# Retention: input rows multiplied by the decayed scores before the value weights

## The reference

```python
ql, kl, vl = h_lat @ Wq, h_lat @ Wk, h_lat @ Wv      # 256, 256 and 512 columns
kc, vc     = h_ctx @ Wk, h_ctx @ Wv
# chunked scans forward and backward, which come to
S   = [ql @ kc.T , ql @ kl.T] * decay                # 256 x 512, decay from the two rates of the head
ret = S @ [vc ; vl]                                  # 256 x 512
r   = head_rms(ret) * silu(h_lat @ Wg)
```

## Time and profile before

| | us |
|---|---|
| median of 3 runs | 2317.76 |
| lowest and highest | 2315.4, 2329.35 |
| profiled execution, device time | 2323.94 |
| its span in the trace | 2322.1 |
| PE busy in the span | 2205.8 (95%) |
| DVE busy | 464.5 (20%) |
| ACT busy | 344.1 (15%) |
| granted TensorE clock, mean | 0.965 of full |

### The profile page before, as it was taken

The page is one execution under the profiler, slowest core; times in us unless marked ns, Lnnn a source line. Parts: engine busy times, 40 slices in busy tenths (PEclk is TensorE's granted clock), DMA queues, the critical chain, the costliest instruction groups (busy, mean ns, idle before and its releaser), DMA issues.

```text
span 2322.1 us, 22897 instructions
## 1 busy us (share of the span) xinstructions
PE 2205.8 (95%) x9001; PEld 925.5 (40%) x9001; DVE 464.5 (20%) x1021; ACT 344.1 (15%) x515; POOL 53.0 (2%) x64
## 2 busy tenths in 40 slices
PE   8988999999999999999999999999999999999997
PEld 6655433222225444445455533333333333333332
DVE  0124311111112301101034132222222212112113
ACT  1321111111111022210114111111111111111111
POOL 1001100000000000000000010000000000000000
PEclk9969799999999999999999989999999999999999
DMA  9484399999999322124240259999999999999994
GB/s 339 162 326 199 156 429 427 428 429 428 428 429 351 109 91 91 50 86 152 93 149 38 84 215 428 428 428 418 429 428 428 427 422 426 429 423 426 429 421 205
DMA packets 88153, 713.17 MB, mean 307 GB/s; under 512 B 6091, under 2 KB 8384, under 8 KB 50832
## 3 DMA queue, kind: packets, MB, share of 16 engines
q1 hardware_dynamic: 86112, 707.20, 73.8%
q0 software_dynamic: 2000, 5.41, 0.7%
HBM read 711.53 MB, written 1.06 MB: 307 GB/s over the span
## 4 chain that ended last, share of the span: by engine, by line
PE 81%; DMA 13%; ACT 3%; DVE 2%; issue 1%; ACTq 0%; DVEq 0%; SPq 0%; POOLq 0%; POOL 0%
PE bank L678 19%; PE bank L668 17%; PE bank L401 14%; DMA ring<-in_w_up 12%; PE bank L389 4%; PE bank L430 4%; PE bank L648 3%; PE bank L685 3%; PE bank L660 3%; PE bank L417 2%; ACT pool L1314 2%; PE bank L859 1%; PE bank L493 1%; PE bank L653 1%; PE bank L980 1%
## 5 line engine op out<-in xcount | busy, mean ns | idle before, releaser
L668 PE MATMUL bank<-ring,pool 128*64 128x512 f32 x2560 | 593.0, 616 | 26.2 <-DMA ring<-in_w_up 22.7
L678 PE MATMUL bank<-ring,pool 128*64 128x512 f32 x2048 | 448.1, 595 | 0.8 <-DVE pool L1834 0.8
L668 PEld LDWEIGHTS bank<-ring,pool 128*64 128x64 f32 x2560 | 182.0, 141 | 411.6 <-issue 365.8
L401 PE MATMUL bank<-ring,pool 128*128 128x512 f32 (+2 forms) x800 | 333.6, 578 | 5.4 <-DVE pool L1950 3.8
L678 PEld LDWEIGHTS bank<-ring,pool 128*64 128x64 f32 x2048 | 144.4, 137 | 281.5 <-issue 279.9
L401 PEld LDWEIGHTS bank<-ring,pool 128*128 128x128 f32 x800 | 152.3, 191 | 181.2 <-issue 167.5
L1208 ACT ACTIVATE pool<-bank 128x512 f32<-128x512 f32 (+1 forms) x125 | 72.9, 583 | 488.7 <-PE bank L401 174.9
L685 PE MATMUL bank<-pool,junk 64*128 64x512 f32 x400 | 99.4, 615 | 1.4 <-ACT pool L1329 1.4
L1900 DVE TENSOR_SCALAR pool<-bank 128x512 f32<-128x512 f32 x32 | 22.1, 692 | 387.5 <-PE bank L678 387.5
L648 PE MATMUL bank<-pool 128*64 128x512 f32 x384 | 96.5, 624 | 2.7 <-DVE pool L1830 2.7
L1911 DVE COPY junk<-bank 128x256 f32<-128x256 f32 x48 | 20.4, 424 | 389.2 <-PE bank L699 389.2
(11 more groups left out here) (345 smaller groups left out, 1380.2 us busy)
## 6 DMA issues: line engine op xcount, KB each, us to landing
ring<-in_exp_w_gu SPq DMA_DIRECT2D x128, 2048.0 KB, 13.7
ring<-in_exp_w_down SPq DMA_DIRECT2D x64, 2048.0 KB, 9.9
ring<-in_w_gate SPq DMA_DIRECT2D x32, 2048.0 KB, 23.6
ring<-in_w_up SPq DMA_DIRECT2D x32, 2048.0 KB, 25.6
ring<-in_w_down SPq DMA_DIRECT2D x32, 2048.0 KB, 21.4
ring<-in_w_in SPq DMA_DIRECT2D x22, 2048.0 KB, 14.4
ring<-in_ada_w SPq DMA_DIRECT2D x12, 2048.0 KB, 11.4
ring<-in_w_out SPq DMA_DIRECT2D x4, 2048.0 KB, 15.6
```

What stands on the lines that cost most here:

```text
L401: i = mm(ps[:, 0:width], src[:, k, t * P:(t + 1) * P], w[:, k, 0:width], start=(k == 0), stop=(k == w.shape[1] - 1))
L668: i = mm(dst[half[f], :], chunks[kk], weights[j][:, k, f * 512:(f + 1) * 512], start=(kk == 0), stop=(kk == KC - 1))
L678: i = mm(dst[half[f], :], chunks[2 * j + k], weights[j][:, k, at:at + 512], start=False, stop=(j == 3 and k == 1))
```

## The change

Per head, the 512 input rows are multiplied by the decayed scores first (`u`, transposed: 8 chunks of 128 columns of `D`, each over 4 blocks of 128 tokens, moving operand `dec2` of 256 columns), ACT copies `u` to `uT`, and `ro` is `uT` times the value weights (2 tiles of 8 matmuls of 512 columns). The value product `rv` of all 512 tokens is gone.

The input rows are needed with tokens on the partitions: `turn_back` transposes `ctxT` (`hc`) and `latT` (`hl`) back, 16 transposes each, and ACT copies them to `in_rows`. They lie in ring slot 5 for the time of phase `b`, which therefore streams through five slots (`PLACE`); the first expert load of `m2` into that slot waits for the last `u` (`unit_done["rows", 0]`). Gate units come before value units in the stream. The scores of head h+1 and their decays are made ahead of `ro` of head h.

```diff
-            at = (FIRST_SLOT[phase] + n) % SLOTS
+            at = PLACE[phase][n % len(PLACE[phase])]
...
-        rv = [B(7 + i).rearrange("p (j c) -> p j c", j=4) for i in range(2)]
+        uT = [B(7 + i).rearrange("p (k t) -> p k t", k=KC) for i in range(2)]
+        in_rows = ring[:, 5 * SLOT:6 * SLOT].rearrange("p (j d) -> p j d", j=4)
...
         for h in range(RH):
+            unit_b(("rg", h), cols(w2, OFF["rg"] + RV * h, RV), 8, RV)
             unit_b(("rv", h), cols(w2, OFF["rv"] + RV * h, RV), 8, RV)
-            unit_b(("rg", h), cols(w2, OFF["rg"] + RV * h, RV), 8, RV)
...
-        FIRST_SLOT = {"a": 0, "m1": len(units_a), "b": len(units_a), "m2": len(units_a) + len(units_b)}
+        PLACE = {"a": (0, 1, 2, 3, 4, 5), "m1": (2, 3, 4, 5, 0, 1), "b": (2, 3, 4, 0, 1), "m2": (5, 1, 2, 3, 4, 0)}
+        BEFORE = {"a": {}, "m1": {j: ("a", len(units_a) - 6 + j) for j in range(SLOTS)},
+                  "b": {n: ("m1", j) for n, j in enumerate((0, 1, 2, 4, 5))},
+                  "m2": {j: ("b", len(units_b) - 6 + j) for j in range(1, SLOTS)}}
...
+            def turn_back(name, srcT):
+
+                for t in range(TC):
+                    for g in range(2):
+                        ps = open_tile(pe, (name, t, g))
+                        for c in range(4):
+                            i = tp(ps[:, c * P:(c + 1) * P], srcT[:, 4 * g + c, t * P:(t + 1) * P], ident)
+                        filled(i, (name, t, g))
+
             pe.wait_ge(S("ctxT_ready"), 8)
             for u in range(2):
                 n = UB["rk", u]
                 by_columns(("kc", u), "b", n, part("b", n, KC, 512), ctxT, last=False)
+            turn_back("hc", ctxT)
             pe.wait_ge(*stage("xn_ready"))
             transposes("lT", xn_rows, 4)
...
+            turn_back("hl", latT)
             pe.wait_ge(S("rotated"), 4)
             transposes("rkT", rk_rows, 4)
...
-            for h in range(RH):
-                n = UB["rv", h]
-                by_rows([("rv", h, j) for j in range(4)], "b", n, part("b", n, KC, RV), both, RV)
+            def scores(h):
                 for jp in range(2):
                     ps = open_tile(pe, ("S", h, jp))
...
+            scores(0)
+            for h in range(RH):
                 n = UB["rg", h]
                 by_rows([("rg", h, t) for t in range(TC)], "b", n, part("b", n, KC, RV), [(latT, t) for t in range(TC)], RV)
-                pe.wait_ge(S("rv_ready"), 4 * (h + 1))
+                if h == 0:
+                    pe.wait_ge(S("in_rows_ready"), 8)
                 pe.wait_ge(S("ret_weights"), 2 * (h + 1))
+                for g in range(4):
+                    ps = open_tile(pe, ("u", h, g))
+                    for c in range(2):
+                        k = 2 * g + c
+                        for j in range(4):
+                            i = mm(ps[:, c * T:(c + 1) * T], in_rows[:, j, k * P:(k + 1) * P], dec2[:, j, :], start=(j == 0), stop=(j == 3))
+                    filled(i, ("u", h, g))
+                if h + 1 < RH:
+                    scores(h + 1)
+                n = UB["rv", h]
+                landed("b", n)
+                w = part("b", n, KC, RV)
+                pe.wait_ge(S("uT_ready"), 4 * h + 4)
                 for t in range(TC):
                     ps = open_tile(pe, ("ro", h, t))
-                    for j in range(4):
-                        i = mm(ps[:, :], dec2[:, j, t * P:(t + 1) * P], rv[h % 2][:, j, :], start=(j == 0), stop=(j == 3))
+                    for k in range(KC):
+                        i = mm(ps[:, :], uT[h % 2][:, k, t * P:(t + 1) * P], w[:, k, :], start=(k == 0), stop=(k == KC - 1))
                     filled(i, ("ro", h, t))
+                multiplied("b", n, ("ro", h, 1))
...
             def ret_decay(h):
 
-                if h:
-                    act.wait_ge(S("ret_out"), 2 * h)
-                else:
+                if h == 0:
...
+            rows_back("hc", 0)
+            rows_back("hl", 2)
             for cp in range(4):
                 evac(rkT[:, 2 * cp:2 * cp + 2, T:2 * T], ("rkT", cp), two, "rkT_ready", RQK ** -0.5)
...
             for h in range(RH):
-                for j in range(4):
-                    if h >= 2 and j == 0:
-                        act.wait_ge(S("ret_out"), 2 * (h - 1))
-                    evac(rv[h % 2][:, j, :], ("rv", h, j), lambda ps: ps[:, :], "rv_ready")
                 for t in range(TC):
 
                     evac(ret[:, t, h * RV:(h + 1) * RV], ("rg", h, t), lambda ps: ps[:, :], "ret_gate", func=ACT.Silu)
+                for g in range(4):
+                    if h >= 2 and g == 0:
+                        tile(act, ("ro", h - 2, 1))
+                    evac(pairs(uT[h % 2], g), ("u", h, g), two, "uT_ready")
+                if h + 1 < RH:
+                    ret_decay(h + 1)
...
+            weights(0)
+            for h in range(RH):
+                if h + 1 < RH:
+                    weights(h + 1)
```

More of the change, by code:

```diff
@@ L368, in landed @@
             def landed(phase, n):
-                pe.wait_ge(S(f"{phase}_full{n % SLOTS}"), 16 * (n // SLOTS + 1))
+                slots = len(PLACE[phase])
+                pe.wait_ge(S(f"{phase}_full{n % slots}"), 16 * (n // slots + 1))
             def transposes(name, src, pairs, among=8, first=0, at=None):
@@ L851, in _ @@
                     filled(i, ("S", h, jp))
+            scores(0)
+            for h in range(RH):
                 n = UB["rg", h]
                 by_rows([("rg", h, t) for t in range(TC)], "b", n, part("b", n, KC, RV), [(latT, t) for t in range(TC)], RV)
[L854 removed]
+                if h == 0:
+                    pe.wait_ge(S("in_rows_ready"), 8)
                 pe.wait_ge(S("ret_weights"), 2 * (h + 1))
+                for g in range(4):
[11 more added lines that the diff above has]
+                pe.wait_ge(S("uT_ready"), 4 * h + 4)
                 for t in range(TC):
                     ps = open_tile(pe, ("ro", h, t))
[L858 to L859 removed]
+                    for k in range(KC):
+                        i = mm(ps[:, :], uT[h % 2][:, k, t * P:(t + 1) * P], w[:, k, :], start=(k == 0), stop=(k == KC - 1))
                     filled(i, ("ro", h, t))
+                multiplied("b", n, ("ro", h, 1))
+            unit_done["rows", 0] = (S(f"bank_full{tiles['u', RH - 1, 3][0]}"), tiles["u", RH - 1, 3][1] + 1)
             for u in range(2):
@@ L1048, in stream, with experts @@
             def stream(phase, units, free):
+                slots = len(PLACE[phase])
                 for n, (src, k, f) in enumerate(units):
-                    if n >= SLOTS:
-                        sp.wait_ge(*unit_done[phase, n - SLOTS])
+                    if n >= slots:
+                        sp.wait_ge(*unit_done[phase, n - slots])
                     elif free:
-                        sp.wait_ge(*free[n])
-                    sp.dma_start(part(phase, n, k, f), src).then_inc(S(f"{phase}_full{n % SLOTS}"), 16)
+                        sp.wait_ge(*free[BEFORE[phase][n][1]])
+                    sp.dma_start(part(phase, n, k, f), src).then_inc(S(f"{phase}_full{n % slots}"), 16)
                     if phase == "a" and n == 1:
                         sp.dma_start(cst[:, P:], consts[:, P:]).then_inc(S("ld_const"), 16)
-            def experts(m, before_, units):
+            def experts(m):
                 E, NB = MOE[m]
                 for j, src in enumerate(moe_units(m, 0)):
-                    sp.wait_ge(*unit_done[before_, len(units) - SLOTS + j])
+                    if m == "m2" and j == 0:
+                        sp.wait_ge(*unit_done["rows", 0])
+                    else:
+                        sp.wait_ge(*unit_done[BEFORE[m][j]])
                     sp.dma_start(moe_slot(m, j), src).then_inc(S(f"{m}_full{j}"), 16)
@@ L1077, in _ @@
             stream("a", units_a, None)
-            stream("b", units_b, experts("m1", "a", units_a))
-            experts("m2", "b", units_b)
+            stream("b", units_b, experts("m1"))
+            experts("m2")
             for t in range(TC):
@@ L1380, in _, with rows_back @@
                     evac(rkT[:, 4 * u + 2 * mp_:4 * u + 2 * mp_ + 2, 0:T], (("kc", u), mp_), two, "rkT_ready", RQK ** -0.5)
+            def rows_back(name, j0):
+                for t in range(TC):
+                    for g in range(2):
+                        evac(in_rows[:, j0 + t, g * 512:(g + 1) * 512], (name, t, g), lambda ps: ps[:, :], "in_rows_ready")
+            rows_back("hc", 0)
+            rows_back("hl", 2)
             for cp in range(4):
@@ L1986, in _, with weights @@
             rss = stat[:, 36:44]
-            for h in range(RH):
+            def weights(h):
                 dve.wait_ge(S("ret_decays"), h + 1)
```

2 lines of the change are left out of this document (removed).

## The result

The median of six runs is 2301.18 us (2300.45 to 2307.3) after, against 2320.38 (2315.4 to 2329.35) before. The ratio is 0.9917, 95% interval 0.9902 to 0.9933: 19.2 us less, at a range of 0.7 to 1.0%. The forecast was 2297, with 22.5 us less as its sum. All medians here leave out two executions that were slow as a whole, one of the kernel before (3809.17 us) and one of the last experiment's (8759.09 us).

A forecast was written before the change was run, and what follows sets the result against it. The retention was taken as PE-bound at full clock. Terms -27.2 + 1.8 + 2.0 + 0.9 = -22.5 us gave 2295.3 to 2301.4 from different baselines; the median was put at 2297, range 2286 to 2308.

The forecast's parts named there:

- Heads: Retention heads: `rv` and old `ro` replaced by `u` and new `ro`, 6.81 us less per head, 27.2 for four.
- the rival of the dearer records: Records of 256 columns in `u` cost more than half of 512-column ones; gain only 5.9 us; chance 0.04.
- `hc`: Sixteen transposes between context keys and `lT`, not hidden by any PE wait: +1.8 us.
- `hl`: Sixteen transposes between `rq` and `rkT`; ACT's twelve copies make PE go on later: +2.0 us.
- The wait for `uT`: After the last head, `ro` waits for ACT's last copy of `u`, with nothing to hide it: +0.9 us.
- The clock: Around the retention: no new fall of the granted clock, a gain of 19 to 27 us; chance 0.73.
- new pauses lower the clock: Rival: joined pause before first scores and the 0.9 us one cause two falls, 3.4 us; gain 19.1; chance 0.2.
- Five slots: Phase `b` ring with five slots instead of six: costs nothing, between 0 and 14 us if a unit were late.
- Decays: Decays in all heads are ready before PE wants them, covered by 8 us in head 0: no cost.
- The expert loop of `m2`: Rival: more slow rounds there, up to 28.7 us lost, making the kernel slower than before at 2324; chance 0.02.
- The odds: Whole kernel: faster by over 1% 0.42, within 1% 0.55, slower 0.03.
- The remark that about 1% can just be told from none: Whole-kernel measurement: a change of 1%, 23.2 us, is about what can be told from none.

The follow-up runs named there:

- the last experiment: Against the changed kernel with both transpose blocks moved: useless matmuls before `rk` and `br`, first `gr` tile ahead of the last `ro`; 2292.11 us, ratio 0.9876.

## Why the prediction was right, and where it was off

The sign, the range (2286 to 2308) and the kind of change were right; the median lies 4 us above the point. By the terms, on the stretch:

- *Heads*, -27.2: measured -27.15 (a head every 44.73 us in place of 51.52). The steady cost of 256-column records decided it, and the rival of the dearer records, with 16.6 us at stake, fell. One of the arguments against that rival misread the code: `u` has its stationary operand in the ring and its moving one in the pool exactly like the keys' product, not the reverse, which makes that row a closer match than was said.
- *`hc`*, +1.8: 1.74 (from the keys' start to `rk`'s, 35.19 us against 33.45).
- *`hl`*, +2.0: 2.25 (from the end of `rq` to the first use of `rqT`, 821.97 - 812.73 against 821.53 - 814.54), by ACT's twelve copies.
- *The wait for `uT`*, +0.9: 1.02 (the last head's `u` and `ro` take 28.56 us from start to start, 13.81 + 13.73 without a wait); 0.78 of it is idle time.
- *The clock*: this is the step that failed. The forecast took the sum without a fall and gave the rival "new pauses lower the clock" 0.2. It is what happened, in both traces of the changed kernel: 2.75 us. With 0.15 that the fall at `rk` was smaller than before, -27.15 + 1.74 + 2.25 + 1.02 + 2.75 - 0.15 = -19.5, the whole of the stretch. The rival's 19.1 was the time to forecast, but in part by luck. Two errors of its working nearly cancel: the price came from the fall at `rk`, 1.7 us, and the one at the scores is 2.75; and it counted a second fall at the 0.78 us pause, where there is none. Neither it nor the sum had the fall at `br`, 1.7 us, which the changed kernel's trace has and the trace before had not.

The reason for holding it unlikely was that two pauses of 1.49 and 1.62 us with 32 transposes had left the clock up. The runs show why that was weak evidence: two short pauses are not one long one. The forecast itself had the two join into one of some 3 us, and for one long pause the trace of before had two rows: 3.81 us at `rk`, with a fall, which the rival quotes, and 2.93 us at `br`, without one, which the prediction doesn't weigh. A pause of 3.1 lies between them, so 0.2 had little ground. The rule of the Trainium skill that was weighed (TensorE: Matmul & The Clock Gate, "Part 4: PE-mode transpose", transposes don't count as busy like matmuls) pointed to the right time; but the runs don't bear it out as the mechanism here. 48 transposes in a row with 1.61 us of pause, 7.3 us in all (814.20 to 821.51), kept the clock, and 32 with 3.81 us lost it.

*Five slots*, nothing: nothing (ratio 1.0005). *Decays*: ready at 830.05 us, 12 us before the first `u` asks for them:

```profile
827.79 0.69 DVE L2032 TENSOR_TENSOR pool<-pool 128x512 f32<-128x512 f32 x1
828.52 1.53 DVE L2035 TENSOR_TENSOR pool<-bank,pool 128x512 f32<-128x512 f32 x2
```

*The expert loop of `m2`*: the chain's 32 rows of this kind (the last one lies behind the loop) hold 14 slow ones before and 14 after, and 14 to 16 in the traces of the ten experiments. The rival needed 14 more to end above before; the count moves by 2. What lies behind the stretch takes 1290.9 to 1297.5 us in the twelve traces (in the last with its early `gr` tile): that is the scatter that a total brings, and the stretch does not.

*The odds.* Faster by over 1% had 0.42 and within 1% had 0.55, which is what came. The remark that about 1% can just be told from none was too wide: the interval of the measured ratio is 0.3% wide in all.

What stays open: why the clock stayed up once behind the 3.81 us pause at `rk` (without the transposes back) and in four traces behind 2.9 us at `br`, and fell twice behind 2.06; why a fall lasts once or twice as long (below); and whether transposes weigh anything at `rk`, which no run separates.

## What to carry to other kernels

Cost a reordering of products by the steady length of a record from the chain, since the group means hide that half the columns cost half. Then list every place where the change joins two short pauses of TensorE into one, and price the clock's fall there: here 2.8 us, against a sum of 22.5. New transposes belong into pauses that exist, and their copies behind those that TensorE waits for, or on an engine that is idle then: the same change with its 32 transposes moved gained 6 us more on the stretch.

## What was not expected of the hardware

The granted clock of the changed kernel sank to half, 1.2 GHz, inside the 3.54 us pause and not behind it: in pieces of 2 us it reads 0.68 from 820, 0.50 from 822 and 824, 0.61 from 826 and 1.00 from 828 us.

Behind pauses of the same length the loss differed: 2.8, 2.7, 2.8, 1.6 and 1.7 us at the scores, 0 to 3.0 us at `rk`. The granted clock in pieces of 1 us accounts for these sizes. In the 22 falls of the table the clock stayed at half for 3.4 us (16 times) or for 6.8 us (6 times), and the product lost half of what lay behind the pause, within 0.05 us. At the first scores of the changed kernel the clock was low for 6.8 us, 1.25 of them still in the pause: half of 5.6 is 2.8. With `hc` alone moved, it was low for 3.4 us, 0.2 of them in the pause: 1.6. Which of the two lengths comes no run here explains.

Two useless matmuls (1.88 us) in a pause of 2.06 stand before an `rk` without a fall in the one trace taken; that they were the reason isn't shown.
